# Conv blocks of a two-model transformer stack: up units as 512-column products with split halves

## The reference, cut to what matters

```python
def conv_ffn(x, w_up, conv_w, conv_b, w_down):
    h = x @ w_up                                   # (256, 1024) @ (1024, 5632)
    c = h.shape[-1]
    h = lax.conv_general_dilated(                  # causal, width 3, one filter per channel
        h, conv_w[:, None, :].astype(h.dtype), window_strides=(1,),
        padding=[(CONV_WIDTH - 1, 0)], dimension_numbers=('NWC', 'WIO', 'NWC'),
        feature_group_count=c) + conv_b
    a, u = jnp.split(h, 2, axis=-1)
    return (jax.nn.gelu(a, approximate=True) * u) @ w_down
...
        h = conv_ffn(rms_norm(x, norm_g[l, 2]), w_up[l], conv_w[l], conv_b[l], w_down[l])
        x = x + rms_norm(h, norm_g[l, 3])
```

## Time and profile before

| | us |
|---|---|
| median of 3 runs | 1359.71 (1358.79 to 1360.68) |
| the profiled execution | 1359.3 |
| its span in the trace | 1357.6 |
| PE busy | 1323.1 (97%), 10001 products |
| PEld busy | 1171.5 (86%) |
| VectorE busy | 978.0 (72%) |
| ScalarE busy | 728.7 (54%) |
| GpSimd busy | 45.7 (3%) |
| share of the chain that ended last | PE 89%, VectorE 6%, ScalarE 3%, issue 2% |

### The profile page before, as it was taken

One profiled execution on the slowest core, in us unless ns is written; L12 is line 12 of the kernel. 1 busy time (PEld: TensorE's weight loads), 2 busy tenths in 40 slices (PEclk: granted clock), 3 DMA queues, 4 the chain that ended last, 5 costly groups with the idle time before them and its releaser, 6 DMA issues.

```text
span 1357.6 us, 24841 instructions
## 1 busy us (share of the span) xinstructions
PE 1323.1 (97%) x10001; PEld 1171.5 (86%) x10001; DVE 978.0 (72%) x1431; ACT 728.7 (54%) x1131; POOL 45.7 (3%) x89
## 2 busy tenths in 40 slices
PE   7999989999999999999999999999999999999999
PEld 7878888999998889999978998888887888888887
DVE  7988886877787678777774767766665857766664
ACT  6853326655567467555565645544444655554442
POOL 6000001000000000000000000100001000000000
PEclk9999999999999999999999999999999999999999
DMA  9511029755544245555556546555553550565530
GB/s 283 189 61 34 20 65 309 244 185 188 184 146 149 86 156 186 186 185 186 169 207 205 168 159 211 193 193 195 193 181 107 181 186 32 174 220 193 188 125 31
DMA packets 136995, 222.38 MB, mean 164 GB/s; under 512 B 6297, under 2 KB 107905, under 8 KB 136640
## 3 DMA queue, kind: packets, MB, share of 16 engines
q1 hardware_dynamic: 134608, 214.32, 47.8%
q0 software_dynamic: 2144, 6.61, 1.5%
q10 hardware_dynamic: 144, 0.06, 0.0%
HBM read 219.90 MB, written 1.05 MB: 163 GB/s over the span
## 4 chain that ended last, share of the span: by engine, by line
PE 89%; DVE 6%; ACT 3%; issue 2%; DMA 0%; DVEq 0%; ACTq 0%
PE ps L573 86%; DVE ulo L559 1%; PE ps L959 1%; PE ps L1377 1%; ACT xn L1656 1%; DVE more L559 0%; DVE x_sb L2192 0%; DVE xs L2184 0%; ACT uhi L551 0%; DVE scratch L2541 0%; DMA scratch<-in_mu 0%; PE ps L1156 0%; DVE scratch L2652 0%; PE ps L1536 0%; DVE gb L2382 0%
## 5 line engine op out<-in xcount | busy, mean ns | idle before, releaser
L559 DVE TENSOR_TENSOR ulo<-raw,uhi 128x1024 fp32r<-128x1024 f32 x243 | 293.3, 1224 | 132.7 <-ACT uhi L551 131.8
L551 ACT ACTIVATE uhi<-raw 128x1024 fp32r<-128x1024 f32 x243 | 252.7, 1053 | 146.4 <-PE ps L573 145.6
L573 PE MATMUL ps<-xn,uhi 128*128 128x256 f32 (+1 forms) x1456 | 308.2, 304 | 2.1 <-ACT xn L1656 1.2
L573 PEld LDWEIGHTS ps<-xn,uhi 128*128 128x128 f32 x1456 | 235.3, 191 | 16.3 <-ACT xn L1656 2.2
L559 DVE TENSOR_TENSOR more<-raw,more 128x1024 fp32r<-128x1024 f32 x152 | 183.6, 1224 | 82.2 <-ACT more L551 81.5
L573 PE MATMUL ps<-xn,ulo 128*128 128x256 f32 x856 | 238.6, 282 | 0.0
L573 PE MATMUL ps<-xn,more 128*128 128x256 f32 (+1 forms) x1624 | 229.2, 299 | 1.2 <-ACT xn L1656 1.2
L573 PEld LDWEIGHTS ps<-xn,more 128*128 128x128 f32 x1624 | 212.7, 191 | 12.9 <-ACT xn L1656 2.1
L551 ACT ACTIVATE more<-raw 128x1024 fp32r<-128x1024 f32 x152 | 158.3, 1054 | 87.5 <-PE ps L573 86.2
L573 PE MATMUL ps<-uhi,xn 128*128 128x512 f32 x536 | 170.5, 393 | 3.5 <-DVE ulo L559 2.5
L573 PEld LDWEIGHTS ps<-xn,ulo 128*128 128x128 f32 x856 | 162.4, 191 | 0.7
(11 more groups left out here) (313 smaller groups left out, 1536.5 us busy)
## 6 DMA issues: line engine op xcount, KB each, us to landing
raw<-in_mlp_w SPq DMA_DIRECT2D x64, 1024.0 KB, 5.3
raw<-in_w_up SPq DMA_DIRECT2D x44, 1024.0 KB, 5.1
raw<-in_w_down SPq DMA_DIRECT2D x22, 1024.0 KB, 4.9
raw<-in_gmlp_w_in SPq DMA_DIRECT2D x16, 1024.0 KB, 5.4
raw<-in_fox_w_in SPq DMA_DIRECT2D x16, 1024.0 KB, 5.1
raw<-in_w_rkv SPq DMA_DIRECT2D x12, 1024.0 KB, 6.8
raw<-in_gmlp_w_out SPq DMA_DIRECT2D x8, 1024.0 KB, 4.9
raw<-in_w_q SPq DMA_DIRECT2D x4, 1024.0 KB, 5.3
```

What stands on the lines that cost most here:

```text
L551: nc.scalar.activation(ring_unit(uhi, m, n), raw_unit(n, j), ACT.Copy).then_inc(hi_done, 1)
L559: nc.vector.tensor_tensor(ring_unit(ulo, m, n), raw_unit(n, j), ring_unit(uhi, m, n).bitcast(F32), ALU.subtract).then_inc(lo_done, 1)
L573: return nc.tensor.matmul(o, l, r, start=start, stop=stop, skip_group_check=True)
```

## The change

Both conv blocks use the wide units. Each pass fills all of banks 4 to 7: part 0 has banks 4 and 5, part 1 has 6 and 7, one unit a bank, with the high half in columns 0 to 255 and the low half in 256 to 511. ScalarE copies the low halves of a part's two banks into a scratch tile C_L (`lows`), VectorE adds the high halves to it into C_U (`halves`), and GpSimd multiplies C_U in place by `tokscale` (`conv_scales`), which VectorE did before out of the bank. up(p) waits for `halves` of pass p - 1. In ScalarE's and VectorE's queues the split of one unit moves ahead of the taps.

```diff
-        def u_unit_wide(pe, m, o):
+        def u_unit_wide(pe, m, o, i=None):
-            pe.wait_ge(lo_done, m + 1)
+            pe.wait_ge(lo_done, (0 if i is None else 12 * i) + m + 1)
...
+            def conv_scales(l):                      # GpSimd
+                pool.wait_ge(spread_done, 1 + 2 * l)
+                for q in range(NP1):
+                    for part in range(2):
+                        pool.wait_ge(halves_done, 2 * (l * NP1 + q) + part + 1)
+                        u = f3(S(C_U + 512 * part, 512))
+                        nc.gpsimd.tensor_tensor(u, u, tokscale[:, :].unsqueeze(1).to_broadcast([P, 2, T]), ALU.mult)\
+                            .then_inc(scaled_done, 1)
...
             row(gb[:, 2, :], g[1, 3:4, :], gb_in[2])
+            conv_scales(0)
             pool.wait_ge(tr_done, 4 * 3)
...
                     for part in range(2):            # TensorE, up(p)
-                        if p >= 2:
-                            pe.wait_ge(scaled_done, 2 * k + 2 * (HP0 + p) - 3 + part)
-                        outs = [bank(4 + 2 * (p % 2) + part, T, T * j) for j in range(2)]
+                        if p >= 1:
+                            pe.wait_ge(halves_done, 2 * k + 2 * (HP0 + p) - 1 + part)
+                        outs = [bank(4 + 2 * part + j) for j in range(2)]
                         if p == 0 and part == 0:
-                            u_units_first(pe, m, outs, xn_hi, xn_lo, split, xhi_done, xlo_done,
-                                          lambda: norm_rest(1 + 2 * l))
+                            u_units_first(pe, m, [o[:, 0:T] for o in outs], xn_hi, xn_lo, split, xhi_done, xlo_done,
+                                          lambda: norm_rest(1 + 2 * l), low_outs=[o[:, T:2 * T] for o in outs])
                             continue
                         for j in range(2):
-                            u_unit(pe, m + 2 * part + j, outs[j], xn_hi, xn_lo, i)
+                            u_unit_wide(pe, m + 2 * part + j, outs[j], i)
...
+                def lows(q, i=None):                 # ScalarE
+                    u, k = (0, 0) if i is None else (12 * i, 2 * i)
+                    m = m0 if q == 0 else m0 + 4 + 6 * (q - 1) if q < NP1 - 1 else m0 + 6 * NP1 - 10
+                    for part in range(2):
+                        act.wait_ge(unit_done, u + m + 2 * part + 2)
+                        if q >= 1 or i is not None:
+                            act.wait_ge(halves_done, 2 * k + 2 * (HP0 + q) - 1 + part)
+                        b = 4 + 2 * part
+                        two = ps[:, 512 * b:512 * b + 1024].rearrange("p (j h t) -> p j h t", h=2, t=T)
+                        A_(f3(S(C_L + 512 * part, 512)), two[:, :, 1, :], ACT.Copy).then_inc(low_done, 1)
...
                     u0 = m0 + 4 + 6 * (p - 1)
+                    lows(p - 1, i)
+                    split_hi(act, u0 + 4, i)
                     taps(p - 1, i)
-                    split_hi(act, u0 + 4, i)
                     gelu(p - 1, i)
...
+                def halves(q, i=None):               # VectorE
+                    k = 0 if i is None else 2 * i
+                    for part in range(2):
+                        dve.wait_ge(low_done, 2 * k + 2 * (HP0 + q) + 1 + part)
+                        b = 4 + 2 * part
+                        two = ps[:, 512 * b:512 * b + 1024].rearrange("p (j h t) -> p j h t", h=2, t=T)
+                        TT(f3(S(C_U + 512 * part, 512)), two[:, :, 0, :], f3(S(C_L + 512 * part, 512)), ALU.add)\
+                            .then_inc(halves_done, 1)
...
-                    dve.wait_ge(unit_done, u + m)
-                    for part in range(2):
-                        scaled(S(C_U + 512 * part, 512), bank(4 + 2 * (q % 2) + part)).then_inc(scaled_done, 1)
...
                     u0 = m0 + 4 + 6 * (p - 1)
+                    halves(p - 1, i)
+                    split_lo(dve, u0 + 4, i)
                     taps(p - 1, i)
-                    split_lo(dve, u0 + 4, i)
                     prod(p - 1, i)
...
                 for q, ends in FFN_TAIL:             # VectorE; ScalarE alike with lows and split_hi
+                    halves(q)
+                    split_all(split_lo, dve, m0, ends[0])
                     taps(q)
-                    split_all(split_lo, dve, m0, ends[0])
                     prod(q)
```

More of the change, by code:

```diff
@@ L48 @@
 SCRATCH = 16392
-C_A, C_B, C_G, C_H, C_U = 0, 512, 1024, 1536, 2048
+C_A, C_B, C_G, C_H, C_U, C_L = 0, 512, 1024, 1536, 2048, 3072
 W_Q, W_KZ, W_KD, W_V = 2048, 4096, 6144, 7168
@@ L408, in build @@
         sum_done = sem("sum_done")
+        low_done = sem("low_done")
+        halves_done = sem("halves_done")
         prod_done = sem("prod_done")
@@ L904, in _ @@
                 .then_inc(aux_in, 16)
+            conv_scales(1)
             pool.wait_ge(unit_done, unit0(at["gv"]) + 1)
@@ L1882, in conv_ffn @@
                 for q, ends in FFN_TAIL:
+                    lows(q)
+                    split_all(split_hi, act, m0, ends[0])
                     taps(q)
-                    split_all(split_hi, act, m0, ends[0])
                     gelu(q)
@@ L2524, in conv_ffn @@
                 c_ = [S(C_A, 512).rearrange("p (f t) -> p f t", t=T), S(C_B, 512).rearrange("p (f t) -> p f t", t=T)]
-                def taps(q, i=None):
-                    u, k, c = (0, 0, 0) if i is None else (12 * i, 2 * i, 4 * i)
-                    m = m0 + 4 if q == 0 else m0 + 8 + 6 * (q - 1) if q < NP1 - 1 else m0 + 6 * (NP1 - 1)
-                    dve.wait_ge(unit_done, u + m)
-                    for part in range(2):
-                        scaled(S(C_U + 512 * part, 512), bank(4 + 2 * (q % 2) + part)).then_inc(scaled_done, 1)
+                def halves(q, i=None):
[6 more added lines that the diff above has]
+                            .then_inc(halves_done, 1)
+                def taps(q, i=None):
+                    k, c = (0, 0) if i is None else (2 * i, 4 * i)
                     for back in (1, 2):
```

## The result

| | before | changed |
|---|---|---|
| median of 4 runs each, us | 1360.0 (1358.79 to 1360.68) | 1372.26 (1371.42 to 1374.66) |
| ratio, 95% interval | 1 | 1.0091 (1.0079 to 1.0103) |
| profiled execution, us | 1359.3 | 1374.66 |
| its span, us | 1357.6 | 1372.7 |
| its mean granted clock | 0.999 | 0.993 |

The changed kernel is slower by 12.3 us. The forecast said slower, by 5.1 us, at most 9.8; so the sign held, and the size is well outside the range.

What follows compares the result with a forecast made beforehand. TensorE's products were taken to bound the kernel (86% of the chain). -4.6 (products) + 5.7 (starts of blocks) + 4.0 (last passes) = +5.1 us on 1359.71 gave 1364.8 us, range 1361.0 to 1369.5.

Steps and rivals of the forecast that it cites:

- The bound: Conv loop: PE is busy for all of each 16.98 us step, so a product saved there is time saved.
- part 1: Up units, passes 1 to 10 of both blocks: fewer, wider products take 352 instead of 360 ns a block; 4.6 us gained.
- not slower: Rival, up units: a block of products takes 333 ns, 17.3 us gained for 9.7 lost, 1352.1 us; chance 0.07.
- no gain: Rival, up units: blocks stay at 360 ns, something other than the number of products paces them; +9.7, 1369.4 us; chance 0.06.
- Part 2: Start of each conv block: pass 1 waits for VectorE's sum of pass 0, 3.8 and 1.9 us late; 5.7 us lost.
- Parts 3 and 4: Loop: sums cost nothing, margin 2.4 us; GpSimd's product takes 1.2 us (0.6 to 2.4), GpSimd and VectorE's splits exclude each other.
- No blocking: Rival: GpSimd and VectorE pass by each other, last passes 1.2 us longer each; +3.5, 1363.2 us; chance 0.18.
- GpSimd bounds VectorE: Rival, loop: GpSimd's blocking raises VectorE's busy time from 13.0 to 17.7 us a step; 1382 us; chance 0.06.
- Part 5: Last pass, behind its last up unit's end (T): VectorE's queue starts taps and out_norm 2.0 us later; 4.0 us lost in two blocks.
- The clock: Rival, first block's start: half clock for some 3.4 us behind the 3.8 us wait costs 1.7; 1366.5 us; chance 0.13.

Runs made afterwards that it cites:

- e5_again: Second measurement of the changed kernel with unread products added on TensorE ahead of pass 1 and down(10) in both blocks: 1369.66 us, ratio 1.0071.
- mix: Changed kernel with wide products only in passes 1 to 8 of each conv block; passes 0, 9 and 10 as before: 1357.86 us, ratio 0.9979.
- e1_wait: Kernel before, with only one wait added per conv block: pass 1 waits for VectorE's tokscale product of pass 0: 1368.89 us, ratio 1.0058.
- e2_head: Changed kernel with the low copy and sum of pass 0, part 0, ahead of the four splits: 1367.47 us, ratio 1.0049.
- e3_order: Changed kernel with the splits back behind the taps in ScalarE's and VectorE's queues: 1368.68 us, ratio 1.0055.
- e6_all: Changed kernel with early sum of pass 0 part 0, splits behind taps, and tokscale product by VectorE from SBUF; all passes wide: 1363.59 us, ratio 1.0016.
- e5_fill: Changed kernel with unread products added on TensorE ahead of pass 1 and of down(10)'s wait in both blocks: 1372.29 us, ratio 1.0083.
- e4_vscale: Changed kernel with the tokscale product made by VectorE from SBUF behind the two sums, none by GpSimd: 1368.61 us, ratio 1.0060.
- e5t: Changed kernel with unread products added on TensorE only ahead of down(10)'s wait in the two last passes: 1371.94 us, ratio 1.0091.
- e5h: Changed kernel with unread products added on TensorE only ahead of pass 1 in the two blocks: 1369.69 us, ratio 1.0064.

## Why the prediction was wrong

**The bound and part 1, the products: right in kind, 0.6 us too good.** The loop's step is 16.80 us against 16.75 forecast, PE-bound. With the clock at full (e5_again) block 1 gives 196.76 - 191.59 - 3.80 - 3.55 = -2.2 and block 2 gives 194.88 - 191.26 - 1.93 - 3.55 = -1.9; 4.0 us for 20 passes, against 4.6. Mix, where nothing is subtracted, gives 0.18 a pass, which would be 3.6. The rivals "not slower" and "no gain" are out. By the start cost that the Trainium skill has (TensorE: Matmul & The Clock Gate, Back-to-back issue gap) it would have been an estimate of 1.6; the runs stand nearer to the rows of the MLP blocks.

**Part 2, the wait at the start: right.** +3.80 and +1.93 against 3.8 and 1.9. e1_wait makes 3.66 and 1.75 of it with nothing else changed. What part 2 did not see is that the hidden half of pass 0 would have been late anyway (e2_head).

**Parts 3 and 4, the loop and GpSimd: right.** No PE idle in the loop. GpSimd's product takes 1.29 us alone, between the bounds and near the 1.2 taken, which was a bracket between far rows (0.6 to 2.4) and so partly luck. The figure of the Trainium skill (GPSIMD Engine Reference, Elementwise: side-by-side cycle accounting) led to an estimate of 1.1. That GpSimd's products and VectorE's splits keep each other waiting is seen in both directions (2.28 and 1.94 us) and is gone in e3_order. "No blocking" and "GpSimd bounds VectorE" are out.

**Part 5, the last pass: mis-sized, 2.0 forecast, 3.55 measured, twice.** The step that failed is "the sum at T + 0.67 to 1.35, GpSimd from T + 1.4 to 2.6", and with it "ScalarE's taps of the second half end at 3.5 and hide" and "All the rest follows at its old distance". It counted one of GpSimd's products behind T, as if the first had been made before. VectorE, with two splits in its queue, comes to the first sum at T + 0.97, so both sums and both products lie behind T: GpSimd runs from T + 1.74 to T + 5.26. VectorE's first tap still started only 2.2 us later than before (T + 4.03 against T + 1.87), close to the 2.0 forecast. That agreement is partly chance: the forecast had the second product in front of the split, where it was the first, somewhat later. What the forecast left free is the rest. The second product holds up the first two taps (1.91 us for 0.95), and the taps of the second half wait for it: ScalarE ends its own at T + 6.2, VectorE all of its taps 3.6 us later than before (at T + 8.7 against T + 5.1). From there all follows at its old distance, and out_norm starts 3.6 us later (T + 17.6 against T + 14.1). e3_order takes 1.1 us off, e6_all 1.7; 1.9 stays with splits still in the queue at T and the sums ahead of the products. Both blocks: 3.1 us of the miss.

**The clock: the term that the sum left out.** It stood among the rivals with 0.13, once, for 1.7 us. In the profiled execution it came four times, for 1.3 to 1.6 us each (1.35 and 1.56 in the blocks, 1.33 twice outside), 5.6 us in all. e1_wait shows that the wait alone brings it, e5_fill and e5_again that it does not come at the heads and at down(10) when TensorE works through the wait. Behind the waits of 3.66 to 3.75 us at the head of block 1 it came in each of the six profiles that had one (changed twice, e1_wait, e3_order, e4_vscale, e5t).

What stays open is why an idle stretch of 1.5 to 2.2 us brings it in one execution and not in another. Behind pass 1 of block 2 it came in the changed kernel at first (1.85 us idle) and in e3_order (1.84), not when the changed kernel ran again (1.84), nor in e4_vscale (1.84), e5t (1.85) or e1_wait (1.75). Eight last passes had the wait of 2.15 to 2.17 us at down(10): right behind it the half clock came in four (the changed kernel again in block 1, e2_head in both, e5h in block 1), in three it came at the norm's transposes instead, and in one, e5h in block 2, not at all. Behind the transposes (1.5 to 1.6 us idle) it also came in e5_again after block 1 and in e5_fill after block 2, with down(10)'s wait filled, and not in e3_order, e4_vscale, e5t or e6_all. No experiment here took one of these stretches apart further.

By these terms: -4.0 + 5.7 + 7.1 = +8.8 us without the clock, against +5.1 forecast. (The -4.0 is itself what is left of two stages of e5_again, so that the sum is closed by it; with mix's 3.6 it would be +9.2.) In the profiled execution 8.8 + 5.6 of half clock + 0.7 of a later start is the whole difference of 15.1. For the medians the difference to the 11.6 and 12.3 measured, 2.8 and 3.5 us, is put down to the clock by the lower mean of these runs (0.993 to 0.996 against 0.997 to 0.999 in the kernel before), not by a trace of each. The forecast missed by 7.5 us: 3.1 the last passes, 0.6 the products, 0.3 the median of before, which came out higher, and about 3.5 that is left to the clock.

## What to carry to other kernels

Where a loop is bound by TensorE, cheaper products pay in its middle, and a longer chain behind them is paid at both ends, where nothing hides it; keep the short form in the first and last passes and take the wide one between (mix: -2.9 us, where all wide is +12.3). When counting the last pass, start each engine from what its queue still holds at T, not from T. And price a new wait of TensorE of 2 to 4 us at up to 1.6 us more than its length (2.2 in e3_order, where the stretch was twice as long); less where PE's next work has a wait in it anyway (0.5 behind down(10)).

## What the runs showed of the hardware

- In each of the six profiles with a wait of TensorE of 3.66 to 3.75 us, a stretch at the lower clock (granted 0.50) began between 1.7 us before the wait's end (e3_order) and 1.5 us behind it (e5t), and lasted 3.4 us (6.8 in e3_order). At idle stretches of 1.5 to 2.2 us it came in some profiles and not in others, of one and the same kernel too. Such a stretch of 3.4 us cost 1.0 us of time in e1_wait, where part of it lay in the wait, 1.3 to 1.6 where it stood alone, and 0.5 where the work behind it had a wait of its own (1.54 us, then 0.30).
- GpSimd's product of two 128x512 fp32 operands, one of them read as a broadcast, took 1.27 to 1.30 us, and 2.25 to 2.28 beside a VectorE split, which grew itself from 1.22 to 1.94 in the last pass. The duration in the profile includes the waiting, so a long VectorE row can be a GpSimd row's doing.
- Kernels that are the same up to the first conv block reached it at 222.5 to 229.1 us. Differences of 2 us between whole times are better read from stages than from medians.
